# Feed-forwards: the product's buffers 64 bytes further, at 256 bytes (modulo 512) from the down weights in place of 192

## What is computed

```python
def swiglu(x, w_gate, w_up, w_down):
    return (jax.nn.silu(x @ w_gate) * (x @ w_up)) @ w_down
...
for l in range(DEPTH):
    x = x + 0.5 * swiglu(rms_norm(x, norm_ffn1[l]), w_ffn1_gate[l], w_ffn1_up[l], w_ffn1_down[l])
    x = x + hybrid_mixer(rms_norm(x, norm_mix[l]), w_in[l], ...)
    x = x + 0.5 * swiglu(rms_norm(x, norm_ffn2[l]), w_ffn2_gate[l], w_ffn2_up[l], w_ffn2_down[l])
```

## The kernel before

| tensor | column | base | address modulo 512 |
|---|---|---|---|
| hT (ffn; also mixer_T_parts) | 32 | first | 128 |
| gate and up parts, first slot | 13296 | first | 448 |
| act (ffn) | 4128 | first | 128 |
| down parts (ffn) | 35440 | first | 448 |
| arrived_down (ffn) | 6176 | first | 128 |
| act (conv_ffn) | 30432 | second | 128 |
| down parts (conv_ffn) | 14512 | second | 448 |
| merged_parts | 14480 | second | 320 |
| mix_parts | 30416 | second | 64 |
| mixer_parts, slots 0 and 2 | 27248, 31344 | first | 448 |

## Time and profile before

### The profile page before, as it was taken

How to read it: one execution, slowest core, us unless ns; L and a number is a source line. 1 busy time by engine, 2 the same in 40 slices (tenths; PEclk the granted TensorE clock), 3 DMA queues, 4 the chain that set the end, 5 groups by cost and what they waited for, 6 DMA issues and landing times. The chain is left out here.

```text
span 2010.8 us, 40869 instructions
## 1 busy us (share of the span) xinstructions
PE 1969.8 (98%) x17166; PEld 1827.0 (91%) x17166; DVE 1348.1 (67%) x2078; ACT 1012.5 (50%) x1477; POOL 13.0 (1%) x14
## 2 busy tenths in 40 slices
PE   8999999999999999999999999999999999999998
PEld 8999987999999998799989989989998989999997
DVE  6554776754755477675558776678766966578775
ACT  6333666533633366653346544456446654356443
POOL 0000000000000000000000100000000010000000
PEclk9999999999999999999999999999999999999999
DMA  8445532644464554164354424366534423366551
GB/s 313 191 193 179 189 138 103 254 188 174 159 243 188 170 184 153 69 254 196 146 200 150 140 85 142 127 250 241 190 137 179 141 96 127 122 203 253 190 188 53
DMA packets 79585, 346.63 MB, mean 172 GB/s; under 512 B 21200, under 2 KB 30544, under 8 KB 45776
## 3 DMA queue, kind: packets, MB, share of 16 engines
q1 hardware_dynamic: 79440, 344.51, 46.8%
HBM read 343.44 MB, written 1.05 MB: 171 GB/s over the span
## 5 line engine op out<-in xcount | busy, mean ns | idle before, releaser
L88 PE MATMUL bank<-ffn_hT_split,n_split_gate_up 128*128 128x256 f32 x1280 | 354.3, 277 | 0.0
L89 PE MATMUL bank<-ffn_hT_split,n_split_gate_up 128*128 128x256 f32 x1280 | 353.8, 276 | 0.0
L90 PE MATMUL bank<-ffn_hT_split,n_split_gate_up 128*128 128x256 f32 x1280 | 353.7, 276 | 0.0
L89 PEld LDWEIGHTS bank<-ffn_hT_split,n_split_gate_up 128*128 128x128 f32 x1280 | 240.5, 188 | 1.5
L88 PEld LDWEIGHTS bank<-ffn_hT_split,n_split_gate_up 128*128 128x128 f32 x1280 | 240.4, 188 | 1.5
L90 PEld LDWEIGHTS bank<-ffn_hT_split,n_split_gate_up 128*128 128x128 f32 x1280 | 240.3, 188 | 0.0
L419 ACT ACTIVATE work<-bank 128x256 f32<-128x256 f32 x88 | 32.8, 382 | 281.2 <-PE bank L90 276.7
L2054 DVE TENSOR_TENSOR mix_parts<-mix_arrived,mix_parts 128x1024 fp32r<-128x1024 f32 x88 | 107.6, 1223 | 86.0 <-ACT mix_parts L2049 85.9
L561 DVE TENSOR_TENSOR work<-bank,work 128x256 f32<-128x256 f32 x88 | 37.2, 422 | 179.0 <-ACT work L419 179.0
L542 DVE TENSOR_TENSOR ffn_split_down<-ffn_arrived_down,ffn_split_down 128x2048 fp32r<-128x2048 f32 x44 | 100.8, 2291 | 79.2 <-ACT ffn_split_down L400 79.2
L2049 ACT ACTIVATE mix_parts<-mix_arrived 128x1024 fp32r<-128x1024 f32 x88 | 92.9, 1057 | 102.9 <-PE bank L90 86.7
(11 more groups left out here) (453 smaller groups left out, 5874.5 us busy)
## 6 DMA issues: line engine op xcount, KB each, us to landing
arrived_gate_up<-in_ffn SPq DMA_DIRECT2D x64, 1024.0 KB, 8.4
ffn_arrived_down<-in_ffn SPq DMA_DIRECT2D x44, 1024.0 KB, 4.8
mix_arrived<-in_mix_w SPq DMA_DIRECT2D x88, 512.0 KB, 3.4
rrived_gate_up<-in_conv_ffn SPq DMA_DIRECT2D x32, 1024.0 KB, 6.7
_arrived_gate_up<-in_ffn SPq DMA_DIRECT2D x24, 1024.0 KB, 6.6
onv_ffn_arrived_down<-in_conv_ffn SPq DMA_DIRECT2D x22, 1024.0 KB, 4.8
mixer_arrived<-in_w_in SPq DMA_DIRECT2D x20, 1024.0 KB, 4.9
irst_project_arrived<-in_w_in SPq DMA_DIRECT2D x17, 1024.0 KB, 5.0
```

The costliest lines, as they stand in the source:

```text
L88: pe.matmul(out, lhs[0], rhs[0], start=start, stop=False)
L89: pe.matmul(out, lhs[0], rhs[1], start=False, stop=False)
L90: return pe.matmul(out, lhs[1], rhs[0], start=False, stop=stop)
```

## The change

The product's buffers move by 16 columns (64 bytes) in both maps, to 192 modulo 512. In the first map the landing buffer of the down weights, which lay right behind them, moves by 128 columns (512 bytes). It now ends 128 columns inside the second half of w_cmp1, and the wait before the load of that half is for the last split of the down weights instead of the last split of gate and up.

```diff
--- before.py
+++ after.py
@@ -817,7 +817,7 @@
     def at(name, col, shape, dtype=F32):
         return nc.alloc_sbuf_tensor_at(name, shape, dtype, offset=FIRST_BASE + 4 * col)
 
-    c.ffn = FfnMemory(at, "ffn", dict(hT=32, act=4128, arrived_down=6176, arrived=(blocks(9200, 2), blocks(23152, 2)),
+    c.ffn = FfnMemory(at, "ffn", dict(hT=32, act=4144, arrived_down=6304, arrived=(blocks(9200, 2), blocks(23152, 2)),
                                       parts=(blocks(13296, 2, 2), blocks(27248, 2, 2)), down_parts=blocks(35440, 2, 2)))
     c.hT_parts = at("mixer_T_parts", 32, [P, 2, KT, S], F32R)
     c.wc1 = at("w_cmp1", 4128, [P, 2, CJ, CMP_HID])
@@ -1028,7 +1028,7 @@
                 for kv in range(2):
                     sp.dma_start(c.pos[:, kv, :], pos[kv].rearrange("(j u) d -> (u d) j", u=2),
                                  allow_slow_non_contiguous=True).then_inc(s["pos_loaded"], 16)
-                sp.wait_ge(prev["gu_split"], before["gu_split"] + 2 * N_CHUNK)
+                sp.wait_ge(prev["down_split"], before["down_split"] + N_CHUNK)
                 sp.dma_start(c.wc1[:, 1], w_c1[1].rearrange("(j p) n -> p j n", p=P)).then_inc(s["wc1_loaded"], 16)
                 for kv in range(2):
                     for u in range(2):
@@ -2012,7 +2012,7 @@
     c.half_parts = [at(f"mix_parts{n}", col, [P, 2, HALF_UNIT], F32R) for n, col in enumerate((30416, 32464, 24272))]
     c.y_rw_parts = at("rw_T_parts", 7208, [P, 2, 4, S], F32R)
     c.merged_parts = at("merged_parts", LOCAL, [P, 2, KT, S], F32R)
-    c.conv_ffn = FfnMemory(at, "conv_ffn", dict(hT=18656, act=30432, arrived=(blocks(8240, 2), blocks(26320, 2)), arrived_down=12368,
+    c.conv_ffn = FfnMemory(at, "conv_ffn", dict(hT=18656, act=30448, arrived=(blocks(8240, 2), blocks(26320, 2)), arrived_down=12368,
                                                 parts=(blocks(48, 2, 2), ((36656, 38704), (24240, 40752))),
                                                 down_parts=((14512, 16560), (32560, 34608)), taps=22752))
```

## The result

The changed kernel takes 2032.01 us (median of 4 runs, 2030.73 to 2034.23) where the kernel before takes 2013.62 beside it (4 runs, 2011.91 to 2014.52): a ratio of 1.0092, with an interval of 1.0081 to 1.0104. It is slower by 0.9%, 18.4 us. The profiled execution took 2031.71 us with a span of 2029.9 us, where before had 2012.56 and 2010.8.

What follows compares the result with a forecast made beforehand. The prediction took TensorE as the bound, busy 1969.8 of 2010.8 us, with matmul pitch deciding. Its terms, 3.2 us saved on down matmuls and 0 elsewhere, took 2013.9 to 2010.7 us, range 2007.6 to 2015.1.

Steps and rivals of the forecast that it cites:

- Part 1: Down matmuls: product moved by 64 bytes makes each of 528 triples 7 ns shorter, 3.7 us less.
- The first rival: Down matmuls: the address distance isn't what makes 687 ns a triple out of 680; time stays 2013.9 us; chance 0.21.
- Part 2: Start of each down phase: settling in loses 8 ns a chunk, leaving 48 ns in 66 chunks, 3.2 us.
- Part 3: Gate and up matmuls after each down phase: nothing of theirs moves, pace left as it is, 0.
- Part 4: Down weights' landing buffer moves 512 bytes, same residue: 0 for the splits and the DMAs.
- part 5: SyncE's wait before w_cmp1's load: w_cv issued about 1.2 us later, covered by 4.5 us before w_in's next unit; cost 0.
- The second rival: Gate and up matmuls stay in the slow pace after each down phase: 409 ns in 54 chunks, 2032.8 us; chance 0.14.
- The third rival: Gate and up matmuls start fast after each down phase: 23 ns in 54 chunks, 1.2 us more gained, 2009.5 us; chance 0.13.
- the rule: Skill text on TensorE's independent read ports, set against the forecast: product's move gains 0, time stays 2013.9 us.

Runs made afterwards that it cites:

- the first experiment: Changed kernel with the product's buffers back at 192 bytes from the down weights, landing buffer and SyncE's wait left as changed: 2014.64 us beside 2014.46 before, ratio 1.0003.
- the fifth experiment: Changed kernel, first block: last product pieces of each down phase moved from 256 to 384, 320 or 288; untimed, down plus gate and up 5497+10889, 5500+11307, 5497+10889, 5537+10890 ns.
- the sixth experiment: Changed kernel with gate and up at 384 or 352 from hT in places, product at 256, 192 or 224; untimed, gate and up 11390, 11393 or 11516 ns where moved.
- the ninth: Changed kernel, first block's last two triples' product moved 16 to 128 bytes in low, high or both parts, second block at 192; untimed, 5466+11307, 5515+11305, 5440+11306, 5490+10897 ns.
- tenth experiments: Changed kernel, first block's high and low product parts at different distances (256, 192, 384), second block at 192; untimed, 5550+10897, 5537+10897, 5547+11307, 5493+11307 ns.

## Why the prediction was wrong

It said 2010.7 us with a range of 2007.6 to 2015.1; the time is 2032.01. By its own steps:

- *Part 1, the product moved by 64 bytes: right.* Triples of 680 ns in place of 687, everywhere in the steady down phases. The first rival, that the address makes no difference, is refuted by the same rows, and the first experiment shows that nothing else in the change does it.
- *Part 2, settling in: a little too careful.* I took 8 ns off each chunk; the steady down phase lost none (54 ns less, 24 pitches of 226.7), and only the first in each feed-forward took 15 ns more. The down matmuls together gave 3.1 us, against 3.2 forecast, but partly by luck: the steady phases gave 2.8 in place of 54 x 48 ns = 2.6, and those at the end of each feed-forward 0.3 in place of 0.6.
- *Part 3, the gate and up matmuls after each down phase: the step that failed.* "The stationary load of the first one still meets the same down weights, so I leave this part as it is: 0." The sentence before it had it right: what decides is how the group is entered, and the change alters what they are entered from. I then let one unchanged pair of operands outweigh that. The runs show that a pace is handed on through the down phase: which one depends on the product's distance over the whole of the phase, its last six matmuls above all, and on the pace in which the phase was entered. The term was +401 ns in 54 chunks, 21.7 us.
- *Part 4, the landing buffer, and part 5, SyncE's wait: right*, both 0 by the first experiment. In the changed kernel w_cv went out 2.3 us after the split's start, as forecast, and the cover before the next unit of w_in was 6.3 us where 4.5 was forecast: the last pair of w_cmp loads took 1.43 us in place of 2.36.
- *The second rival is what happened*, nearly to the number: it priced 409 ns a chunk (measured 401), less 3.2 us (measured 3.1), and gave 2032.8 us (measured 2032.01). It had 0.14. The evidence that I held against it was "all 54 entries from a down phase escape after 5". But all 54 had the same distance, the same instructions and the same predecessors. They were one observation made 54 times, made at the one value that the change would leave. The one different observation that I had, the first 24 gate matmuls slow in the first feed-forward and fast in the fourth at identical addresses, said that both paces are open there, and I should have given the two about even chances. In the changed kernel that same group, still with nothing moved, exchanged its pace in three of the six feed-forwards: 2736 to 2740 ns in the first, fourth and fifth, 2830 to 2833 in the others, where before it was fast in the fourth and sixth.
- *The third rival, a fast start*, didn't occur, though the fifth experiment's phases (10889, one or two slow pitches) show that such a start exists and is worth 17 ns a chunk.
- *The range* is 0.1 us off its own sums, which give 2007.7 and 2015.2; nothing hangs on it.

Of the rule: rows 4 and 6 had shown 687 and 680 ns. The change now shows them for one and the same tensor pair, and the down matmul of 512 columns takes 226.7, 228.9, 232.3 or 233 ns at distances of 256, 192, 384 and 320 (the phase before it has a smaller part: 5439 to 5485 ns for 24 at 256, in the sixth experiment). "TensorE: Matmul & The Clock Gate" of the Trainium skill (Part 2, step by step) has the two operands come through independent read ports, with no bandwidth taken by the next load. It says nothing of addresses, and read so, all of these would be equal, as the prediction had it. The measurement decides: for these fp32r matmuls with a load before each they are not.

What stays open is what is handed over. The last pitch of the down phase goes with it in most cases (232 or more is followed by the fast pace, 229 or less by the slow one), but 230 to 231 is followed by either (before: fast; product at 224: slow), 234 by slow in the ninth and tenth experiments, and with four transposes in between the relation is turned round: 232 to 237 before a slow phase, 228 to 231 before a fast one. What puts the matmuls ahead of the first down phase into one pace or the other, differently from one run to another, is open too. The trace has a start and a length for each matmul and no state of the ports, so I name no mechanism below that.

## What to carry to other kernels

Where TensorE is the bound and never idle, a layout that makes one group of matmuls faster has to be judged with the group that follows it, since the pace can be handed on; a trial that moves only the last pieces of the operand shows whether the two can be had apart. Count as evidence only observations that differ in what the change alters: fifty equal repeats at the old setting say nothing of how firm it is. And when a pace shows two values at the same addresses anywhere in a trace, price both and assume for neither that it stays as it is.

## What the runs showed of the hardware that I had not expected

- In the two pairs tried, the distance between stationary and moving operand acts modulo 256 bytes, not 512: 448 gave exactly 192's times, 0 exactly 256's. Moving the last piece 16 bytes from 256 changed nothing; 32 did.
- Two paces for the same matmuls at the same addresses, 113.3 and 117.8 ns for 256 columns, each held to the end of its phase: at 117.8 ns the 96 never recovered in 54 chunks, and at 113.3 ns it took none to five pitches to settle. In the slow pace one of three weight loads takes 192 ns in place of 188, and it can be the first, the second or the third.
- The down phase can have two paces too: at 192, with gate and up at 320, it takes 5494 ns entered fast and 5600 entered slow, and leaves the gate and up phase fast both times.
- The pace can alternate from chunk to chunk in a regular way (5588+11311, 5600+10901 and again), with periods of two and of four chunks seen, and the whole pattern can be shifted by a chunk between two feed-forwards that run the same instructions.
- High and low part at 256 and 192, or the other way round, made the down phase slower (5537 to 5550) than both parts at either (5440, 5494).
